# Dilated attention with its bias tiles loaded in the projection stage, queries and keys loaded over all partitions, and values loaded in two parts

## The reference

```python
DILATED_PATTERNS = ((128, 1), (512, 4), (2048, 16))     # window, dilation; 8 heads of 64
proj = rmsnorm(x, g_attn_norm) @ w_in                   # q_a, k_a, v_a: 512 columns each, and the latents
for window, dilation in DILATED_PATTERNS:
    # each query attends to keys i + j*dilation, |j| <= window // (2*dilation)
    scores = q . k * 64 ** -0.5 + rel_bias[bucket(distance)]
    o, lse = softmax(scores) @ v, log_sum_exp(scores)
w = softmax(stack(lses))                                # over the three patterns
out_a = sum(w * outs)
```

## Time and profile before

| | us |
|---|---|
| median of 3 runs | 2899.21 (2895.56 to 2911.0) |
| the profiled execution | 2902.9, its span 2901.1 |
| PE busy | 2224.9 (77%) |
| DVE busy | 1336.9 (46%) |
| ACT busy | 1022.6 (35%) |
| POOL busy | 534.2 (18%) |

### The profile page before, as it was taken

How to read it: one execution, slowest core, us unless ns; L and a number is a source line. 1 busy time by engine, 2 the same in 40 slices (tenths; PEclk the granted TensorE clock), 3 DMA queues, 4 the chain that set the end, 5 groups by cost and what they waited for, 6 DMA issues and landing times. The chain is left out here.

```text
span 2901.1 us, 34464 instructions
## 1 busy us (share of the span) xinstructions
PE 2224.9 (77%) x12244; PEld 1836.5 (63%) x12244; DVE 1336.9 (46%) x2217; ACT 1022.6 (35%) x1809; POOL 534.2 (18%) x628
## 2 busy tenths in 40 slices
PE   6992975599969499996299997688397999464248
PEld 5881974499957266664178885577386888354137
DVE  4401652555544466664622112577464211375753
ACT  4400652355432155553321110345343111453331
POOL 0000000432011121221200004234130000464122
PEclk8995987799979599998599998788698999777669
DMA  5519965633044479983652213312444211221133
GB/s 198 214 46 193 209 141 182 164 95 79 12 164 138 153 306 366 361 337 149 239 185 77 80 48 98 89 44 51 139 138 160 83 70 51 83 66 32 47 138 102
DMA packets 223745, 400.74 MB, mean 138 GB/s; under 512 B 99168, under 2 KB 119008, under 8 KB 210672
## 3 DMA queue, kind: packets, MB, share of 16 engines
q1 hardware_dynamic: 175904, 300.50, 34.0%
q10 hardware_dynamic: 37664, 79.44, 7.2%
q0 software_dynamic: 10032, 18.90, 1.7%
HBM read 305.92 MB, written 110.66 MB: 144 GB/s over the span
## 5 line engine op out<-in xcount | busy, mean ns | idle before, releaser
L78 PE MATMUL pe_acc<-pe_w,hT 128*128 128x512 f32 x960 | 219.8, 392 | 8.7 <-DVE pe_w L197 8.7
L78 PEld LDWEIGHTS pe_acc<-pe_w,hT 128*128 128x128 f32 x960 | 181.5, 189 | 46.9 <-DVE pe_w L197 9.1
L78 PE MATMUL ex_gu<-hT,ex_xT 128*128 128x512 f32 x792 | 195.6, 403 | 0.8 <-DVE hT L1902 0.8
L1902 DVE TENSOR_TENSOR hT<-ex_raw,hT 128x2048 fp32r<-128x2048 f32 x66 | 150.9, 2287 | 87.9 <-ACT hT L1873 85.9
L78 PE MATMUL pg_acc<-hT,pg_w 128*128 128x512 f32 x768 | 176.1, 392 | 8.5 <-DVE pg_w L197 8.5
L78 PEld LDWEIGHTS ex_gu<-hT,ex_xT 128*128 128x128 f32 x792 | 148.5, 191 | 34.7 <-DVE hT L1902 1.2
L78 PEld LDWEIGHTS pg_acc<-hT,pg_w 128*128 128x128 f32 x768 | 144.8, 189 | 39.6 <-DVE pg_w L197 9.5
L1873 ACT ACTIVATE hT<-ex_raw 128x2048 fp32r<-128x2048 f32 x66 | 126.1, 1913 | 41.6 <-PEq L47 23.9
L262 DVE COPY pe_o<-pe_acc 128x512 f32<-128x512 f32 x28 | 19.4, 691 | 239.5 <-PE pe_acc L78 239.5
L1194 PE MATMUL ab_op<-ab_v,ab_pT 128*128 128x64 f32 x1024 | 121.3, 272 | 0.0
L1831 PE MATMUL ex_dn<-ex_wd,ex_hT 128*128 128x512 f32 x264 | 118.7, 593 | 0.8 <-ACT ex_hT L1867 0.8
(11 more groups left out here) (455 smaller groups left out, 5214.4 us busy)
## 6 DMA issues: line engine op xcount, KB each, us to landing
ex_raw<-in_w_gate SPq DMA_DIRECT2D x33, 1024.0 KB, 7.2
ex_raw<-in_w_up SPq DMA_DIRECT2D x33, 1024.0 KB, 11.2
ex_wd<-in_w_down SPq DMA_DIRECT2D x33, 1024.0 KB, 14.0
hT<-scr_qk SPq DMA_DIRECT2D x96, 256.0 KB, 7.7
scr_qk<-pa_parts ACTq DMA_DIRECT2D x32, 512.0 KB, 3.8
pe_raw<-in_even_w_in SPq DMA_DIRECT2D x6, 2048.0 KB, 7.9
pg_raw<-in_odd_w_in SPq DMA_DIRECT2D x5, 2048.0 KB, 8.7
e_e<-scr_y SPq DMA_DIRECT2D x16, 512.0 KB, 10.6
```

The lines of the kernel that those rows point to most:

```text
L78: mm = pe.matmul(out, a(p, k), b(q, k), start=(k == 0 and i == 0), stop=(k == n - 1 and i == 2))
L1902: dve.tensor_tensor(split(s, LO)[:, :, g, :], raw[:, s % NW, g, :].rearrange("p (k n) -> p k n", k=8), split(s, HI)[:, :, g, :].bitcast(F3 ...
```

## The change

- `project` takes a callback `also(sp)`, called on SP behind the load of chunk 1. A new class `Biases`, opened in a stage around both `project` and `dilated_attention`, uses it to load one near tile (128 x 8 x 256) and the far one (128 x 8 x 384). The near tiles for the first and last tile of queries are made in the attention stage by GpSimd (two memsets, two copies into `be`), and VectorE waits for them (`edges` 4) at its first tile.
- `parts` no longer has memory of its own but lies over `obuf`; ACT and VectorE wait for all of its stores before the first chunk that isn't split.
- Queries and keys: the moving side `kn`, `ka` holds the keys' high part in partitions 0 to 63 and the low part in 64 to 127, loaded by one DMA for each order; `q2` holds the queries' high part twice, loaded by one DMA from a source repeated with `to_broadcast`; `ql` holds their low part in 64 partitions. The second product of each order takes 64 rows (queries' low part by keys' high part). The product of both low parts is no longer computed. There are 6 DMAs for each head instead of 12.
- Values: the columns of heads 0 and 1 are loaded ahead of head 1's queries and keys, the others behind them; TensorE waits for the first part at the first value product and for the second at the first of head 2.

```diff
-        parts = st.sb(name + "_parts", [P, 2, 2, 2, BANK], F32R) if cut else None
+        parts = obuf[:, :, :].rearrange("p (x o a) n -> p x o a n", x=2, o=2).bitcast(F32R)
...
+                    if g == 1 and also:
+                        also(sp)
...
+                    if cut and g > 0 and "split" in chunks[g - 1] and "split" not in ch:
+                        for u in range(2):
+                            act.wait_ge(cut_out[u], 16 * cuts[g])
...
+class Biases:
+    def __init__(self, st, table):
+        self.table = table
+        self.near = st.sb("bi_near", [P, 8, QW])
+        self.apart = st.sb("bi_apart", [P, 8, QW + P])
+        self.loaded = st.sem("bi_loaded")
+
+    def load(self, sp):
+        row = lambda at, w: bass.AP(self.table.tensor, at, [[1, P], [2 * BANK, 8], [1, w]])
+        sp.dma_start(self.near[:, :, :], row(0, QW)).then_inc(self.loaded, 16)
+        sp.dma_start(self.apart[:, :, :], row(BANK, QW + P)).then_inc(self.loaded, 16)
...
-        qs = store[:, 0:4 * S].rearrange("p (u o s) -> p u o s", u=2, o=2)
...
-        bn = st.sb("aa_bn", [P, 3, HN, QW])
-        ba = st.sb("aa_ba", [P, HN, QW + P])
+        q2, ql = (store[:, 4 * S * n:4 * S * (n + 1)].rearrange("p (u o s) -> p u o s", u=2, o=2) for n in range(2))
+        kn = store[:, 8 * S:8 * S + 2 * W].rearrange("p (u s) -> p u s", u=2)
+        ka = store[:, 12 * S:14 * S].rearrange("p (u s) -> p u s", u=2)
+        be = st.sb("aa_be", [P, 2, HN, QW])
...
-                    for o, (hi, lo, at) in enumerate(((kh, kl, DV), (gh, gl, 0))):
-                        for b in range(2):
-                            sp.dma_start(qs[64 * b:64 * b + 64, u, o, :].bitcast(F32), qk[o, b, h * DV:(h + 1) * DV, :]).then_inc(qk_in[u], 16)
-                            for a, dst in enumerate((hi, lo)):
-                                sp.dma_start(dst[64 * b:64 * b + 64, u, at:at + S].bitcast(F32), qk[o, a, 512 + h * DV:512 + (h + 1) * DV, :]).then_inc(qk_in[u], 16)
+                    for o, k in enumerate((kn[:, u, DV:DV + S], ka[:, u, :])):
+                        q_rows, k_rows = (slice(512 * x + h * DV, 512 * x + (h + 1) * DV) for x in range(2))
+                        sp.dma_start(k.bitcast(F32), qk[o, :, k_rows, :]).then_inc(qk_in[u], 16)
+                        sp.dma_start(q2[:, u, o, :].bitcast(F32),
+                                     qk[o, 0, q_rows, :].unsqueeze(0).to_broadcast([2, DV, S])).then_inc(qk_in[u], 16)
+                        sp.dma_start(ql[0:DV, u, o, :].bitcast(F32), qk[o, 1, q_rows, :]).then_inc(qk_in[u], 16)
+
+                def load_v(c0, c1, sem):
+                    cc = slice(c0, c1)
+                    vr = v_src.rearrange("(t p) n -> p t n", p=P)
+                    sp.dma_start(vn[DV:P, 0:NT, cc], vr[0:DV, :, cc]).then_inc(sem, 16)
+                    sp.dma_start(vn[0:DV, 1:NT + 1, cc], vr[DV:P, :, cc]).then_inc(sem, 16)
+                    for a in range(2):
+                        sp.dma_start(va[:, 4 * a:4 * a + 4, cc],
+                                     v_src[a * BANK:(a + 1) * BANK].rearrange("(p g) n -> p g n", g=4)[:, :, cc]).then_inc(sem, 16)
...
                 load_qk(0)
...
                 sp.wait_ge(pads_in, 2)
...
+                load_v(0, 2 * DV, v0_in)
                 load_qk(1)
+                load_v(2 * DV, 512, v_in)
...
-                        pe.matmul(sps[T % 3][:, 0:QW], qs[:, u, 0, ii], kh[:, u, i * P:i * P + QW], start=True, stop=False)
-                        pe.matmul(sps[T % 3][:, 0:QW], qs[:, u, 0, ii], kl[:, u, i * P:i * P + QW], start=False, stop=True)
...
+                        kk = kn[:, u, i * P:i * P + QW], by_group(ka[:, u, :])[:, :, i % 4, :]
+                        for o in range(2):
+                            s = sps[T % 3][:, o * QW:(o + 1) * QW]
+                            pe.matmul(s, q2[:, u, o, ii], kk[o], start=True, stop=False)
+                            mm = pe.matmul(s, ql[0:DV, u, o, ii], kk[o][0:DV], start=False, stop=True)
+                        mm.then_inc(s_done, 1)
...
+    with stage(nc) as st:
+        bias = Biases(st, scr["table"])
+        project(nc, "pa", hT, 8, [
...
+        ], gain=[(0, A["g_attn_norm"][0])], also=bias.load)
+        dilated_attention(nc, ident, hT, bias, scr["qk"], scr["va"], scr["oa"], scr["oa2"], scr["stat"])
```

More of the change, by code:

```diff
@@ L79, in product, with project @@
     return mm
-def project(nc, name, hT, nk, chunks, gain=None):
+def project(nc, name, hT, nk, chunks, gain=None, also=None):
     N = len(chunks)
@@ L248, in _ @@
                         split_lo(dve, g + 1)
+                    if cut and g > 0 and "split" in chunks[g - 1] and "split" not in ch:
+                        for u in range(2):
+                            dve.wait_ge(cut_out[u], 16 * cuts[g])
                     for j in range(groups(ch)):
@@ L776, with dilated_attention @@
 QW = 2 * P
-def dilated_attention(nc, ident, hT, qk, v_src, table, near, apart, stat):
+class Biases:
[8 more added lines that the diff above has]
+        sp.dma_start(self.apart[:, :, :], row(BANK, QW + P)).then_inc(self.loaded, 16)
+def dilated_attention(nc, ident, hT, bias, qk, v_src, near, apart, stat):
     HN, T8, DV = 8, NT, 64
@@ L875, in _ @@
                 pool.memset(vn[DV:P, NT, :], 0.0).then_inc(pads_in, 1)
+                pool.wait_ge(pads_in, 2)
+                pool.memset(be[:, 0, :, QW - DV:], MASK).then_inc(edges, 1)
+                pool.wait_ge(edges, 1)
+                pool.memset(be[:, 1, :, 0:DV], MASK).then_inc(edges, 1)
+                pool.wait_ge(edges, 2)
+                pool.wait_ge(bias.loaded, 32)
+                pool.tensor_copy(be[:, 0, :, 0:QW - DV], bias.near[:, :, 0:QW - DV]).then_inc(edges, 1)
+                pool.wait_ge(edges, 3)
+                pool.tensor_copy(be[:, 1, :, DV:], bias.near[:, :, DV:]).then_inc(edges, 1)
+                pool.wait_ge(edges, 4)
             @block.tensor
             def _(pe):
-                pe.wait_ge(keys_ok, 4)
+                pe.wait_ge(keys_ok, 2)
                 for T in range(TT + 3):
@@ L928, in _ @@
                         if T == 0:
-                            dve.wait_ge(edges, 2)
-                            dve.wait_ge(bias_in, 64)
+                            dve.wait_ge(edges, 4)
+                            dve.wait_ge(bias.loaded, 32)
                         dve.wait_ge(s_done, T + 1)
@@ L933, in _ @@
                             dve.wait_ge(p_done, 2 * (T - 1))
[L934 to L935 removed]
+                        near_bias = be[:, 0, h, :] if i == 0 else be[:, 1, h, :] if i == T8 - 1 else bias.near[:, h, :]
+                        tile_bias = (near_bias, bias.apart[:, h, (i // 4) * P:(i // 4) * P + QW])
                         for a in range(2):
[L937 removed]
+                            dve.tensor_tensor_reduce(out=sc[:, T % 2, a, :], in0=sps[T % 3][:, a * QW:(a + 1) * QW], in1=tile_bias[a][:, ::-1],
                                                      scale=1.0, scalar=-3e38, op0=ALU.add, op1=ALU.max,
@@ L1339, in first_attention @@
     krv = tiled(w_in)
[L1340 to L1345, removed]
-                             (slice(48, 64), krv[:, :, kr0:kr0 + 16])]),
-    ], gain=[(0, A["g_attn_norm"][0])])
+    with stage(nc) as st:
+        bias = Biases(st, scr["table"])
+        project(nc, "pa", hT, 8, [
+            *(dict(kind="T", width=512, load=columns(w_in, 512 * c, 512), split=heads_to(scr["qk"], 8 * c)) for c in range(2)),
+            dict(kind="row", width=512, load=columns(w_in, 1024, 512), dst=to_rows(scr["va"], 0, 512)),
+            dict(kind="row", width=384, load=columns(w_in, 1536, 384), dst=to_rows(scr["lat"], 0, 384)),
+            dict(kind="T", width=64, dst=to_T(scr["krT"], 0, 64),
+                 load=[(slice(0, 32), krv[:, :, kr0:kr0 + 32]), (slice(32, 48), krv[:, :, kr0 + 16:kr0 + 32]),
+                                 (slice(48, 64), krv[:, :, kr0:kr0 + 16])]),
+        ], gain=[(0, A["g_attn_norm"][0])], also=bias.load)
+        dilated_attention(nc, ident, hT, bias, scr["qk"], scr["va"], scr["oa"], scr["oa2"], scr["stat"])
     heads_of = lambda src, h0=0: lambda h: src[bass.ds(h * 64 + h0, 64), :]
     values_of = lambda src: lambda h: src[:, bass.ds(h * 64, 64)].rearrange("(t p) d -> p t d", p=P)
-    dilated_attention(nc, ident, hT, scr["qk"], scr["va"], scr["table"], scr["oa"], scr["oa2"], scr["stat"])
     norm_rows(nc, "nl", ident, 384, [(0, 384, lambda t: rows(scr["lat"], t))], [(0, 256), (256, 128)], hT=hT)
```

33 lines of the change are left out of this document (8 added, 25 removed).

## The result

| | before | after |
|---|---|---|
| median, us | 2899.03 (4 runs, 2895.56 to 2911.0) | 3130.39 (4 runs, 3124.53 to 3134.14) |
| profiled execution, us (its span) | 2902.9 (2901.1) | 3124.5 (3122.7) |
| first issue of the dilated attention to first issue of the next stage | 201.6 | 427.1 |
| mean granted TensorE clock | 0.862 | 0.825 |

The change makes the kernel 7.9% slower: ratio 1.0788, 95% interval 1.0753 to 1.0824. The forecast was 3102 us with a range of 3045 to 3165. The stage grew by 225.5 us, the span by 221.6; all the rest together moved by 4 us.

A forecast was written before the change was run, and what follows sets the result against it. Transfers bound the dilated attention until 400 us. Start 223.2 + 2 latency + 346 loads + 12 stores + 15 values, then 25.7 + 2.9 + 1, put its end at 628 us: 3106 profiled, 3102 median; range 3045 to 3165.

The forecast's parts named there:

- The loads run on two engines: Dilated attention: the four large query and key loads a head, outermost dimension 2, use 2 DMA engines, not 16; chance 0.81.
- The count of small packets: DMA view: one completion mark per engine taking part; two small packets expected for each large load.
- 43.3 us of loads and 2.3 of stores a head: Dilated attention: engine 0 carries 1.081 MB of loads a head at 25 GB/s, 43.3 us; stores 2.3 us each.
- First score product near 268 us: Sign in the dilated attention: TensorE's first score matmul comes near 268 us instead of 240.
- Last head's load landed at 598: Dilated attention: last head lands at 598 us, from 223.2 + 2 + 346 + 12 + 15.
- 25.7 + 2.9 + 1 us from the last head's first product to the next stage: End of the dilated attention: 25.7 us as before, 2.9 for the low clock, 1 for the added barrier.
- TensorE wait 20 to 30 us for each head: Sign in the dilated attention: six or seven TensorE waits for query and key loads, each 20 to 30 us.
- Small edits: Barrier, early biases, split-store waits, GpSimd copies, fewer memsets and issues: 1 us for the barrier, cost 0 for the others.
- The additional barrier: The new outer stage adds one more clearing and barrier: 0 to 2 us, taken as 1.
- The two GpSimd copies: Attention stage: copies of 128 x 1536 values for the edges, some 7 us for both, hidden beside the first load; cost 0.
- Rest of the kernel constant: Outside the dilated attention: everything stays constant unless the projections before it suffer.
- The faster rival: Dilated attention: loads spread over all 16 engines and TensorE bounds the stage, ending 59 us earlier, 2840 us; chance 0.13.

The follow-up runs named there:

- e6: Kernel before, with each stacked pair of 64-row query and key loads issued as one load of outermost dimension 2, nothing else changed: 3258.72 us.
- e11: Kernel before, with all six stacked loads of a head in the form 4 x 32 x 1024 (not the attention's result): 3051.57 us.
- e5: Changed kernel, its key and high-part query loads kept, queries' low part loaded as 64 x 2 x 1024, second product over 128 rows: 3113.11 us.
- e1: Changed kernel, with each of the four large loads of a head issued as two loads of 64 rows: 3010.29 us, ratio to before 1.0366.
- e3: e1 with the queries' low part loaded twice and the second product over 128 rows: 2867.56 us, ratio to before 0.9870.
- e9: e2 with the queries' low part loaded once, into even partitions, and zeros in the odd ones: 2846.27 us, ratio to before 0.9803.
- e2: Changed kernel, loads sourced 64 x 2 x 1024, queries' low part repeated too, second product over 128 rows: 2852.94 us, ratio to before 0.9834.
- e8: e1 with the four score products ordered 128, 64, 64, 128 rows instead of 128, 64, 128, 64: 2982.78 us.
- e10: e2 with one more product a tile, 64 rows by 8 columns, into a bank nothing reads: 2971.23 us.

## Why the prediction was right

- *The loads run on two engines*: right, and shown by e6 and e11 with the rest of the kernel as it was. The Trainium skill has it as the forecast quoted it (page DMA: Bandwidth & Descriptors, section Why a DMA increments its semaphore by 16 and not by 1): the largest number up to 16 that divides the slowest dimension on both sides. The traces agree at 2 (12.8% and 26 GB/s an engine) and at 4 (about 104 GB/s). The count of small packets, from which the step was argued, reads two a load in e6.
- *43.3 us of loads and 2.3 of stores a head*, 45.6: measured 45.5. The rate of a lone engine was 26 GB/s against the 25 taken.
- *First score product near 268 us*: 273.1. 1.75 us of the difference is the start of the stage, which is late from the first norm on: the projections begin 1.8 us later too (43.35 against 41.56 us). *Last head's load landed at 598*: its first product came at 604.56, 6.6 us later.
- *25.7 + 2.9 + 1 us from the last head's first product to the next stage*: measured 47.5. This is the term that was mis-sized, 18 us, and most of the distance between 3106 forecast for the profiled execution and 3124.5. The step said "the second of each pair has 64 rows in place of 128" and gave it no price; it costs 1.1 us a tile at the low clock, and with it the clock stays low. e5, without it, took 28.4. In the seven heads before, the 36 us of compute lie behind 45 us of loads, as forecast for up to 27, with 9 us to spare (the waits of 8.90 to 10.10 us above), where the forecast had TensorE wait 20 to 30 us for each head; in e5 it waits 28 to 30 from the fourth head on. A cost of about 140 us (e1 against e3) was hidden by a greater one. That the number came out so near is luck in part: the stage ended at 652.0 us, 24 later than the 628 forecast (6.6 in the last load, the rest in this term), and the stages behind it took 5.6 us less.
- *Small edits*: right. From the first product of the projections to the last copy of their outputs are 177.5 us in both profiles (41.56 to 219.12 and 43.35 to 220.87), with the biases' 2.5 MB landing in between; ACT's first row copy comes 5.06 us after the last split stores' issue in both (136.10 to 141.16, 138.27 to 143.33). The additional barrier, taken as 1 us, doesn't show: last store of the statistics to the next stage 4.36 us before (420.42 to 424.78) and 4.34 after (647.69 to 652.03). The two GpSimd copies took 2.9 us together, not 7.
- *Rest of the kernel constant*: 2476.3 us from the next stage's start to the end before (2901.1 - 424.78), 2470.7 after.
- *The faster rival* fell, but its price was wrong too. It had 2840 us if the loads spread over 16 engines. e1 does just that and takes 3010, bound by TensorE from its first head on: the rival forgot the 64-row products. "Faster" stood at 0.13 for a case that by e1 would not have been faster in this form; e9 has both repairs, the loads' form and products of 128 rows, and takes 2846.

## What to carry to other kernels

Write a transfer so that the outermost dimension of both sides is a multiple of 16: here 2 ran on two engines, 4 at the rate of four, 64 and 128 on sixteen. A stack of two parts is a reason to put the part behind the row, not to give up the full width, as long as both operands of the product have the same order of rows. And a smaller product can cost more than a full one where it interrupts a run of products of one shape: doubling its rows was worth 143 us here (e1 to e3), and filling them with zeros did no worse (e9 beside e2). Whether the clock suffers has to be read in the trace of the stage; in the retention layer it did not. Price each edit alone on the engine it touches, also where another limit hides it, since that is what remains when the other limit is lifted.

## What the runs showed of the hardware that was not expected

- A change between a product of 128 rows and one of 64 makes the next weight load wait for the product before it: 0.22 us before the load at 1.2 GHz (e1, e8, and the retention layer of before), and 0.24 us a change in the tile's time (4.49 us with four changes, 4.01 with two).
- With two such changes in every tile of 12 or 13 instructions the granted clock stays at 0.50 as long as the score products last (e8, e10), though the records show PE busy throughout; with none it rises to 1.00 under the same loads and the same engines around it (e2, e9). In the retention layer, with a change after every two products, it is 1.00 all the same. Which property of the stream the clock follows is not settled.
- One DMA engine of two at work moves 26 GB/s of 4 KB rows (e6), as much as one of sixteen does at its best in this kernel (423 GB/s at share 1.01).
- A destination of every second partition costs the load nothing that shows: e9's stage is 7 us shorter than e2's.
